# Where three operand tiles of TensorE begin within a line of 64 bytes

## What is computed

```python
def sq_relu_mlp(h, w1, w2):
    return jnp.square(jax.nn.relu(h @ w1)) @ w2

def swiglu(x, w_gate, w_up, w_down):
    return (jax.nn.silu(x @ w_gate) * (x @ w_up)) @ w_down
```

## The kernel before

| tile | before | after |
|---|---|---|
| WS | 32896 (0) | 32896 (0) |
| HS2 | 57504 (32) | 57552 (16) |
| HTS | 73888 (32) | 73968 (48) |
| X | 97664 (0) | 97792 (0) |
| H | 114048 (0) | 114176 (0) |
| HID | 135808 (0) | 136000 (0) |
| CH | 180864 (0) | 181072 (16) |

## Time and profile before

### The profile page before, as it was taken

How to read it: one execution, slowest core, us unless ns; L and a number is a source line. 1 busy time by engine, 2 the same in 40 slices (tenths; PEclk the granted TensorE clock), 3 DMA queues, 4 the chain that set the end, 5 groups by cost and what they waited for, 6 DMA issues and landing times.

```text
span 2291.0 us, 39244 instructions
## 1 busy us (share of the span) xinstructions
PE 2170.2 (95%) x15820; PEld 1906.7 (83%) x15820; DVE 1499.4 (65%) x2399; ACT 929.2 (41%) x1448; POOL 42.6 (2%) x37
## 2 busy tenths in 40 slices
PE   6999889999989989999999989999999999899998
PEld 2654578888777689999998987799989999687997
DVE  4789664544455766676667784576686676656666
ACT  3224532222234744454444452444454453344444
POOL 0000000000003000000001000000000000000000
PEclk9999999999999999999999998999999999999999
DMA  7768322222222045545554311255545554143553
GB/s 291 266 247 296 109 74 101 92 96 98 92 92 83 20 166 186 188 168 189 186 190 149 122 48 57 101 175 184 186 153 188 187 176 138 56 138 122 192 191 120
DMA packets 93555, 338.87 MB, mean 148 GB/s; under 512 B 10224, under 2 KB 12400, under 8 KB 93168
## 3 DMA queue, kind: packets, MB, share of 16 engines
q1 hardware_dynamic: 92096, 331.84, 41.9%
q10 hardware_dynamic: 1328, 5.21, 0.6%
HBM read 335.96 MB, written 1.05 MB: 147 GB/s over the span
## 4 chain that ended last, share of the span: by engine, by line
PE 86%; DVE 7%; ACT 3%; DMA 2%; issue 1%; SPq 0%; DVEq 0%; ACTq 0%
PE ps L551 21%; PE ps L553 21%; PE ps L552 21%; PE ps L953 2%; PE ps L656 2%; DMA ring<-weights 2%; PE ps L563 1%; PE ps L564 1%; PE ps L1222 1%; PE ps L574 1%; DVE WS L2046 1%; PE ps L1033 1%; DVE RS L2449 1%; PE ps L901 1%; PE ps L1056 1%
## 5 line engine op out<-in xcount | busy, mean ns | idle before, releaser
L2046 DVE TENSOR_TENSOR WS<-ring,WS 128x1024 fp32r<-128x1024 f32 x484 | 593.9, 1230 | 359.9 <-ACT WS L1502 356.4
L1502 ACT CAST WS<-ring 128x1024 fp32r<-128x1024 f32 x484 | 504.8, 1045 | 570.3 <-PE ps L553 474.3
L551 PE MATMUL ps<-HS,WS 128*128 128x256 f32 x1968 | 553.4, 281 | 3.1 <-DVE WS L2046 2.9
L553 PE MATMUL ps<-HS,WS 128*128 128x256 f32 x1968 | 548.7, 279 | 0.0
L552 PE MATMUL ps<-HS,WS 128*128 128x256 f32 x1928 | 538.7, 279 | 0.0
L551 PEld LDWEIGHTS ps<-HS,WS 128*128 128x128 f32 x1968 | 369.8, 188 | 5.3 <-DVE WS L2046 4.3
L553 PEld LDWEIGHTS ps<-HS,WS 128*128 128x128 f32 x1968 | 369.9, 188 | 0.0
L552 PEld LDWEIGHTS ps<-HS,WS 128*128 128x128 f32 x1928 | 362.4, 188 | 1.0 <-issue 1.0
L551 PE MATMUL ps<-HTS,WS 128*128 128x256 f32 x960 | 269.5, 281 | 2.8 <-DVE HTS L2126 1.6
L552 PE MATMUL ps<-HTS,WS 128*128 128x256 f32 x960 | 268.3, 280 | 0.0
L553 PE MATMUL ps<-HTS,WS 128*128 128x256 f32 x960 | 267.5, 279 | 0.0
(11 more groups left out here) (422 smaller groups left out, 3119.3 us busy)
## 6 DMA issues: line engine op xcount, KB each, us to landing
ring<-weights SPq DMA_DIRECT2D x630, 512.0 KB, 3.4
X<-xs ACTq DMA_DIRECT2D x1, 2048.0 KB, 8.8
con<-const ACTq DMA_DIRECT2D x1, 2016.0 KB, 9.5
X<-mem ACTq DMA_DIRECT2D x1, 1024.0 KB, 5.5
y<-X SPq DMA_DIRECT2D x4, 256.0 KB, 2.2
vecs<-vec SPq DMA_DIRECT2D x1, 311.5 KB, 7.5
con<-const SPq DMA_DIRECT2D x1, 130.0 KB, 8.6
```

Source lines behind the costliest of these rows:

```text
L551: pe.matmul(dst, w[0][:, cut], upper, start=first, stop=False, skip_group_check=True)
L553: return pe.matmul(dst, w[1][:, cut], upper, start=False, stop=last, skip_group_check=True)
L1502: act.copy(WS[:, split % HALVES, 0, :], ring[:, panel % RING, :]).then_inc(uppers_ready, 1)
L2046: dve.tensor_tensor(WS[:, split % HALVES, 1, :], ring[:, panel % RING, :], WS[:, split % HALVES, 0, :].bitcast(F32), ALU.subtract).then_in ...
```

## The change

The tiles HS2 and HTS are allocated with 64 bytes more, and the tile is a view that begins 48 or 16 bytes behind the start. HID and CH get 64 bytes more too; HID begins 64 bytes and CH 16 bytes behind the start. The arena's tiles that begin behind CH (SCP, RELU, RELU2, MSQ) move by 32 elements, 128 bytes. `stored`, the view of HID's memory in which YL lies, still begins at the start of the allocation. Everything that is allocated behind HTS moves by 128 bytes. Each engine's instructions, their order, shapes and waits are the same in both programs; only the addresses differ.

```diff
-        HS2 = sb("HS2", 2, KT, T, dt=F32R)
-        HTS = sb("HTS", 2, 2, T, dt=F32R)
+        HS2 = sb("HS2", 2 * KT * T + 16, dt=F32R)[:, 12:12 + 2 * KT * T].rearrange("p (a k t) -> p a k t", a=2, k=KT)
+        HTS = sb("HTS", 2 * 2 * T + 16, dt=F32R)[:, 4:4 + 2 * 2 * T].rearrange("p (a b t) -> p a b t", a=2, b=2)
...
-            HID = convolution.enter_context(nc.sbuf_tensor("HID", [P, 11, 2, 2 * T], F32R))
-            CH = convolution.enter_context(nc.sbuf_tensor("CH", [P, 2, KT, 2 * T], F32R))
+            hidden = convolution.enter_context(nc.sbuf_tensor("HID", [P, 11 * 4 * T + 16], F32R))
+            halves = convolution.enter_context(nc.sbuf_tensor("CH", [P, 4 * KT * T + 16], F32R))
+        HID = hidden[:, 16:16 + 11 * 4 * T].rearrange("p (n a t) -> p n a t", n=11, a=2)
+        CH = halves[:, 4:4 + 4 * KT * T].rearrange("p (a k t) -> p a k t", a=2, k=KT)
...
-        SCP = area(19456, KT, 32)
+        SCP = area(19488, KT, 32)
...
-        RELU, RELU2 = area(19456, 2, 2 * T), area(20480, 2, 2 * T)
+        RELU, RELU2 = area(19488, 2, 2 * T), area(20512, 2, 2 * T)
...
-        MSQ = area(19456, KT, T)
+        MSQ = area(19488, KT, T)
...
-        stored = HID[:, :, :, :].rearrange("p a b c -> p (a b c)")
+        stored = hidden[:, 0:11 * 4 * T]
```

## The result

The changed kernel takes 2313.76 us (two runs, 2313.39 and 2314.14), against 2291.55 before: a ratio of 1.0096, with a 95% interval from 1.0076 to 1.0116. It is slower by 22.2 us, within the range of the prediction but on the other side of before than its forecast. The spans are 2311.3 and 2291.0 us.

The account below looks back on a forecast made before the run. TensorE was taken as the bound, through the steps between matmul starts. Gains of 3.5 us (HS2, HTS) and 4.9 (CH moving) less 1.6 (CH stationary) gave -6.8 from 2291.55: 2284.8 us, range 2240 to 2319.

Parts of the forecast that it names:

- What bounds the kernel: Whole kernel: TensorE, busy 2170.2 of 2291.0 us; only addresses change, so matmul counts times differences of pace give the sum.
- their place in a line is the same. I cost them at nothing: HID moved by one whole line, X, H, con, vecs and the arena's later tiles by two: no cost.
- CH as moving tile: 1456 products with CH moving, lines 563, 564 and 574: 24 cycles in place of 32, 4.9 us gained.
- the middle: Products of lines 551 to 553 with HS2 or HTS moving: all at 116.67 ns, 3.5 us gained.
- CH as stationary tile: Convolution diagonals and value rows, 246 matmuls with CH pieces now crossing a line: 6.67 ns each, 1.6 us lost.
- HS2 as stationary piece: 48 matmuls of lines 1016 to 1018: HS2 was across a line and stays so, no change.
- Rival 3: HS2 and HTS products: only half a line helps, a quarter costs as much as none, 120.0 ns; 2318.8 us; chance 0.09.
- Rival 1: All moved tiles: the address does nothing, the two paces differ for another reason; 2291.5 us; chance 0.17.
- Rival 2: HS2, HTS and CH products: a quarter line removes nearly the whole stall, steps of 0.11 us; 2216.7 us; chance 0.13.
- Rival 4: Every product of the three moving tiles: one more line stalled, 48 cycles in place of 24 to 32; 2386.8 us; chance 0.06.

Follow-up runs that it names:

- the best kernel: HS2 and HTS put at distance 112, HID and CH left at 0, pads of 512 bytes, against the kernel before: 2266.03 us, ratio 0.9879.
- run 118: Not a follow-up run: "run" is a verb here, and 118, 119, 116 are steps in ns between matmul starts at distance 32.

## Why the prediction went wrong

**What bounds the kernel** held: the same instructions and waits, the sum a number of matmuls times a difference of paces, nothing else moved. So did reading starts and not durations, and the counts.

**"their place in a line is the same. I cost them at nothing"** (said of HID and of what lies behind HTS) was the step that failed, and it failed twice. For HID (64 bytes and the shift) it cost 5.1 us. And it hid the shift from CH: I gave CH one displacement of 16 bytes, where it had 16, 64 and 128. The kernel with nothing but the shift shows what such a move costs: 18.2 us in one run, some 15 of them in the four tiles. The reason beneath is that I read the pace off the tile's own place in a line of 64. The rows of before can't tell that from a distance to WS: WS lay on a line and did not move, so 32 and 0 were the place and the distance at once. Of the 29 us between forecast and result CH as moving tile makes about 15, HS2 and HTS together 10, HID 5.

**CH as moving tile**, -4.9 us, came out at +10.1. The 8.0 ns more that were measured lie outside the bounds that I had kept (10 ns less, 6.67 ns more).

**HS2 and HTS at 116.67, "the middle"**, -3.5 us, came out at +17.5 and -11.1. The prediction named this as its test: "if HS2 and HTS should differ from each other". They do, but not because one side of the line counts: 80 and 112 are two places of a scale of 256, and no slope along it led from 0 and 32 to either. That these two partly cancel is why the total lay in the range: that was luck.

**CH as stationary tile**, +1.6 us, did not show. By starts, the products of the value rows stand closer than before, 116.7 ns in the mean for 119.8, and those of the convolution at 233.5 for 232.8; paired with before that is 0.3 us less and 0.1 us more. And HS2 as stationary piece (233.3) is faster by 1.3 ns at its new place, 232.0.

**The rivals.** Rival 3 (2318.8) is nearest in time and had HS2 right at 120.0, but not HTS, and nothing of CH and HID. Rival 1 falls: addresses count, and more than I held. Its argument, two paces at one offset, was a true reading, but it doesn't speak against addresses (last section). Rival 2's pace of 0.11 us was there to be had: the best kernel goes at 113.33, though not at the 110 of that row. Of the distances tried only 112 gives it in nearly every group. Rival 4's form, a fixed extra line per matmul, was not seen.

## What to carry to other kernels

When TensorE is the bound and its products take a stationary and a moving operand from tiles that never move, measure the step between starts against the distance of the two tiles modulo 256 bytes; a pad of a few bytes was worth 1.2% here, and an innocent one of 128 bytes ahead of two others cost 0.8%, in one run. Give a pad a multiple of the period (512 bytes were free here), so that later tiles keep their places, and compute every tile's address before and after, not only those in the diff. Average over a whole cycle of steps, and look at stretches in which the tiles have different shares before one of them is called faster.

## What the runs showed of the hardware

The settled step, by distance from WS modulo 256, is the mean of the last twelve steps in a dense group of more than twenty. Where groups of one kernel settle differently, or two kernels have the distance, all values are given. The 256 columns between the two lengths cost 106.7 ns at distance 0; at this price a matmul of 256 columns costs 106.7 ns in columns alone, one of 512 costs 213.3.

| distance | 256 columns, ns | 512 columns, ns |
|---|---|---|
| 0 | 120.0 | 226.7 |
| 16 | 113.3, 116.7 or 118.5 to 118.8 | 231.7 |
| 32 | 116.7 or 117.8 | 233.3 |
| 48 | 118.3 | 233.3 |
| 64 | 117.8 | 228.9 or 233.3 |
| 80 | 120.0 or 118.3 | 231.1 |
| 96 | 120.0 | 233.3 |
| 104, 108 | 120.0 | |
| 112 | 113.3 (115.0 to 115.5 in a few) | 226.7 or 231.1 |
| 116, 120 | 121.7, 122.2 (120.0 to 120.4 in a few) | |
| 128 | 118.2 to 120.0 | 231.7 to 233.3 |
| 160 | 117.1 to 118.6 | 233.8 to 234.6 |
| 192 | 113.3 or 117.8 | 233.3 |
| 208 | 119.2 to 119.5 | 234.4 to 235.0 |
| 240 | 117.2 | 236.7 or 233.3 |

Different tiles agree at one distance. CH's 192 products of 256 columns, which no run was made for, go at 116.7 and 117.8 at distance 32, at 120.0 and 118.3 at 80, at 113.3 in four of six groups at 112 and at 116.8 to 117.2 at 240, much as HS2 and HTS do there; the entries for 0, 64, 128, 160 and 208 in the middle column are CH's alone.

I had not expected three things. The best place differs by length: distance 0 is the best for 512 columns and among the slow ones for 256. The scale is not smooth: 112 costs 16 cycles beside the columns, 116 costs 36. And a distance can have two or three settled cycles of steps: at 32 the steps run 118, 119, 116 in some stages and 116, 118, 120, 113, 116, 117, 120, 114 in others, which is what the earlier trace rows show. What chooses between them is not shown, but the neighbours have a part in it: with HTS alone moved, all 230 dense groups of HS2 settle at 116.7, where 70 of 229 went at 117.8 before. A settled cycle needs some steps to come about: with HS2 at 32, a group of HTS at 112 begins at 116 to 121 and falls to 113 and 114 in the eleventh step (kernel with HTS alone):

```profile
1111.36 0.28 PE L551 MATMUL ps<-HTS,WS 128*128 128x256 f32 x1
...
1112.55 0.28 PE L552 MATMUL ps<-HTS,WS 128*128 128x256 f32 x1
1112.66 0.28 PE L553 MATMUL ps<-HTS,WS 128*128 128x256 f32 x1
...
1114.02 0.28 PE L553 MATMUL ps<-HTS,WS 128*128 128x256 f32 x1
```

Ten steps of 119 ns in the mean to the second row (1.19 us), then thirteen of 113 to the last (1.47 us). In the changed kernel, with HS2 at 80, all 110 groups of HTS that follow one of HS2 without a break begin at 113 at once.

The runs show that the distance decides, not why. One could think that the load of the next stationary piece and the stream of the moving tile get in each other's way in the memory; that would fit a dependence on distance, but no run shows it, since the profile shows no single read. The Trainium skill (SBUF — State Buffer, Who interferes with whom) gives TensorE two independent read ports, one for the moving operand and one for loading weights. By that rule alone one would expect no dependence on the distance between the two; the runs show one, 113.3 against 120.0 ns at 112 and 96, but not whether the ports have to do with it. The Trainium skill's lines of 16 bytes, each crossing to a new one at a price (SBUF — State Buffer, Specifications), fit in part: off a multiple of 16 the steps are 120.0 to 122.2. But among the multiples of 16 they spread from 113.3 to 120.0 as well. Not tried: other lengths, other stationary layouts, and the distances without an entry.
